# Expert numbers of a routing unit: compare, multiply and sum, against difference and least absolute value

## The reference

```python
q = (xt @ w_query).reshape(t, PEER_HEADS, 2, PEER_HALF)          # 8 heads, two halves of 128
s = jnp.einsum('thpd,hpnd->thpn', q, sub_keys)                   # 128 scores for each half
s_top, i_top = lax.top_k(s, PEER_TOPK)                           # 16 best keys of each half
cand = (s_top[:, :, 0, :, None] + s_top[:, :, 1, None, :]).reshape(t, PEER_HEADS, 256)
c_top, c_idx = lax.top_k(cand, PEER_TOPK)                        # 16 best sums
idx1 = jnp.take_along_axis(i_top[:, :, 0], c_idx // PEER_TOPK, axis=-1)
idx2 = jnp.take_along_axis(i_top[:, :, 1], c_idx % PEER_TOPK, axis=-1)
expert = idx1 * PEER_KEYS + idx2                                 # number of the expert
gate = jax.nn.softmax(c_top, axis=-1)
```

## Time and profile before

| | |
|---|---|
| median of 3 runs | 3614.72 us (3612.92 to 3615.78) |
| span of the profiled execution | 3610.9 us |
| time of the profiled execution | not listed apart from its span; the runs shown lie 2.0 to 4.9 us above that span |
| PE busy | 3447.2 us (95%) |
| DVE busy | 2815.0 us (78%) |
| ACT busy | 1079.8 us (30%) |
| POOL busy | 1422.8 us (39%) |

### The profile page before, as it was taken

One profiled execution on the slowest core, in us unless ns is written; L12 is line 12 of the kernel. 1 busy time (PEld: TensorE's weight loads), 2 busy tenths in 40 slices (PEclk: granted clock), 3 DMA queues, 4 the chain that ended last, 5 costly groups with the idle time before them and its releaser, 6 DMA issues.

```text
span 3610.9 us, 39997 instructions
## 1 busy us (share of the span) xinstructions
PE 3447.2 (95%) x11593; PEld 1976.1 (55%) x11593; DVE 2815.0 (78%) x6484; ACT 1079.8 (30%) x2721; POOL 1422.8 (39%) x1233
## 2 busy tenths in 40 slices
PE   7999999999997999768799999999999999999998
PEld 4666666777774566556344444444444444444443
DVE  2466686776774389899788888987898889888898
ACT  3233344544442222268221112111211121121212
POOL 1000000000001277500566565655666566655665
PEclk9999999999997999989899999999999999999999
DMA  3111013000002234247999999999999999999998
GB/s 112 30 36 35 0 32 109 23 23 29 29 35 114 50 60 91 34 139 203 394 393 377 393 380 392 379 380 356 394 372 387 386 397 377 375 394 377 390 376 340
DMA packets 313936, 829.65 MB, mean 230 GB/s; under 512 B 41504, under 2 KB 145056, under 8 KB 305056
## 3 DMA queue, kind: packets, MB, share of 16 engines
q0 software_dynamic: 165888, 537.01, 39.9%
q1 hardware_dynamic: 125104, 227.45, 17.4%
q10 hardware_dynamic: 22768, 63.18, 4.5%
HBM read 789.73 MB, written 37.81 MB: 229 GB/s over the span
## 4 chain that ended last, share of the span: by engine, by line
PE 46%; issue 5%; DVE 3%; DMA 2%; POOL 1%; ACT 0%; ACTq 0%; DVEq 0%; POOLq 0%
PE peer_ps_o L1971 23%; PE peer_ps_d L1958 20%; PE peer_ps_q L1888 2%; DMA peer_vr<-in_v_rows,peer_index 2%; DVE Y L2196 1%; POOL peer_vr L1863 0%; DVE peer_mt L2156 0%; DVE peer_mt L2160 0%; POOL peer_ur L1856 0%; DVE peer_ur L2185 0%; PE peer_ps_s L1903 0%; DMA peer_ur<-in_u_rows,peer_index 0%; DVE route_hit L1221 0%; DVE peer_chosen L1223 0%; DVE Y L2213 0%
## 5 line engine op out<-in xcount | busy, mean ns | idle before, releaser
L1856 POOL DMA_INDIRECT peer_ur<-in_u_rows,peer_index x512 | 566.1, 1106 | 600.1 <-DVE peer_ur L2185 418.7
L2196 DVE SCALAR_TENSOR_TENSOR Y<-peer_vr,osq,Y 128x1024 f32<-128x1024 f32 x512 | 656.7, 1283 | 100.2 <-DMA peer_vr<-in_v_rows,peer_index 99.8
L1863 POOL DMA_INDIRECT peer_vr<-in_v_rows,peer_index x512 | 588.3, 1149 | 324.9 <-issue 148.2
L2185 DVE SCALAR_TENSOR_TENSOR peer_ur<-peer_ur,Y 128x1024 f32<-128x1024 f32 x512 | 627.6, 1226 | 8.0 <-DMA peer_ur<-in_u_rows,peer_index 8.0
L1958 PE MATMUL peer_ps_d<-hnT,route_ut 128*128 128x512 f32 x1376 | 598.6, 592 | 0.7 <-ACT peer_vr L2031 0.7
L1971 PE MATMUL peer_ps_o<-hw,Y 128*128 128x512 f32 x1024 | 446.2, 595 | 14.8 <-DVE Y L2172 14.7
L1971 PE MATMUL peer_ps_o<-hnT,Y 128*128 128x512 f32 x1024 | 442.6, 592 | 0.0
L1958 PEld LDWEIGHTS peer_ps_d<-hnT,route_ut 128*128 128x128 f32 x1376 | 261.2, 190 | 328.6 <-issue 327.7
L1971 PEld LDWEIGHTS peer_ps_o<-hw,Y 128*128 128x128 f32 x1024 | 194.9, 191 | 257.5 <-issue 235.9
L1971 PEld LDWEIGHTS peer_ps_o<-hnT,Y 128*128 128x128 f32 x1024 | 193.5, 190 | 238.2 <-issue 238.0
L1958 PE MATMUL peer_ps_d<-hnT,peer_ut 128*128 128x512 f32 x672 | 297.3, 595 | 6.7 <-ACT Y L2039 6.7
(11 more groups left out here) (331 smaller groups left out, 5018.8 us busy)
## 6 DMA issues: line engine op xcount, KB each, us to landing
route_ut<-in_u_cols SPq DMA_DIRECT2D x86, 512.0 KB, 7.4
hw<-in_v_cols SPq DMA_DIRECT2D x16, 2048.0 KB, 11.0
peer_mt<-sel ACTq DMA_DIRECT2D x64, 512.0 KB, 9.2
hnT<-in_v_cols SPq DMA_DIRECT2D x16, 2048.0 KB, 13.6
peer_ut<-in_u_cols SPq DMA_DIRECT2D x42, 512.0 KB, 7.3
route_wk<-in_w_route ACTq DMA_DIRECT2D x14, 1024.0 KB, 7.8
hnT<-in_w_route SPq DMA_DIRECT2D x9, 1024.0 KB, 4.8
route_wk<-in_w_route SPq DMA_DIRECT2D x9, 1024.0 KB, 6.9
```

What stands on the lines that cost most here:

```text
L1856: pool.indirect_dma_start(ur[:, r % RING, :], None, u_rows, bass.IndirectOffsetOnAxis(ap=index[:, r // TOPK % 4, r % TOPK:r % TOPK + 1], a ...
L1863: pool.indirect_dma_start(vr[:, r % RING, :], None, v_rows, bass.IndirectOffsetOnAxis(ap=index[:, r // TOPK % 4, r % TOPK:r % TOPK + 1], a ...
L2185: nc.vector.scalar_tensor_tensor(out=ur[:, s, :], in0=ur[:, s, :], scalar=1.0, in1=Y[:, b, D:MIX], op0=ALU.mult, op1=ALU.mult, accum_out=d ...
L2196: nc.vector.scalar_tensor_tensor(out=hb, in0=vr[:, s, :], scalar=hid[:, c:c + 1], in1=hb, op0=ALU.mult, op1=ALU.add).then_inc(comb_done, 1)
```

## The change

The place of a candidate is now written into its number. `APART` is 2 x 128 x 128 = 32768, more than any expert number. Each key number gets a share added: for the first half 32768 times the place at which the key's row of candidates begins (`ROW_START`), for the second half 32768 times its rank. The sum of both is 32768 x place + expert number. `route_experts` then takes 32768 x chosen place less this number. Where the places agree, the absolute value is the expert number; everywhere else it is larger. A reduce by minimum with absolute value picks it out.

Per unit this has one operation over 16 x 54 elements and one reduce, where there were two and one. In `route_keys` two scalar_tensor_tensor over 16 elements stand for one multiply over 32. The buffers `count_u` (54 words) and `wide` go, `shift` (32 words) comes, `hit` is called `apart`. At the start of `mix_out`, 32 memsets of one element fill `shift` in place of two for `wide`, and one iota goes from POOL.

```diff
+ROW_START = [sum((v - u) * w for u, v, w in GRID if v <= i) + r * m for i, j, m in GRID for r in range(j - i)]
+APART = 2 * KEYS * KEYS
...
-        self.count_u = sb("count_u", [P, NCAND], U32)
-        self.wide = hw[:, FIRST_K * D + 4:FIRST_K * D + 6].unsqueeze(2)
-        self.hit = sb("hit", [P, TOPK, NCAND])
+        self.shift = sb("shift", [P, 2, TOPK])
+        self.apart = sb("apart", [P, TOPK, NCAND])
...
-    own.now(nc.vector.tensor_tensor(R.ti[:, 1], R.ix[:], R.wide.to_broadcast([P, 2, TOPK]), ALU.mult))
+    for p in range(2):
+        own.step(nc.vector.scalar_tensor_tensor(out=R.ti[:, 1, p, :], in0=R.ix[:, p, :], scalar=(float(KEYS), 1.0)[p],
+                                                in1=R.shift[:, p, :], op0=ALU.mult, op1=ALU.add))
+    own.hold()
...
 def route_experts(nc, dve, own, R, n, chosen):
-    own.now(nc.vector.tensor_tensor(R.hit[:], R.count_u[:].unsqueeze(1).to_broadcast([P, TOPK, NCAND]),
-                                    R.place[:].unsqueeze(2).to_broadcast([P, TOPK, NCAND]), ALU.is_equal))
-    own.now(nc.vector.tensor_tensor(R.hit[:], R.hit[:], R.ce[:, 1, :].unsqueeze(1).to_broadcast([P, TOPK, NCAND]),
-                                    ALU.mult))
-    return nc.vector.tensor_reduce(chosen, R.hit[:], AX.X, ALU.add)
+    own.now(nc.vector.scalar_tensor_tensor(out=R.apart[:], in0=R.place[:].unsqueeze(2).to_broadcast([P, TOPK, NCAND]),
+                                           scalar=float(APART),
+                                           in1=R.ce[:, 1, :].unsqueeze(1).to_broadcast([P, TOPK, NCAND]),
+                                           op0=ALU.mult, op1=ALU.subtract))
+    return nc.vector.tensor_reduce(chosen, R.apart[:], AX.X, ALU.min, apply_absolute_value=True)
...
-            nc.gpsimd.iota(R.count_u[:], pattern=[[1, NCAND]], base=0, channel_multiplier=0)
...
-            nc.vector.memset(R.wide[:, 0, :], float(KEYS))
-            own.now(nc.vector.memset(R.wide[:, 1, :], 1.0))
+            for a in range(TOPK):
+                nc.vector.memset(R.shift[:, 0, a:a + 1], float(APART * ROW_START[a]))
+                own.step(nc.vector.memset(R.shift[:, 1, a:a + 1], float(APART * a)))
```

## The result

Before: 3613.82 us (median of 4 runs). After: 3594.52 us (median of 4, 3591.34 to 3597.35). The ratio is 0.9945, 95% interval 0.9934 to 0.9957: 19.3 us less, where 3593 was forecast. After measured once more, beside other kernels, gave 3592.03 us and 0.9942 (0.9929 to 0.9956). The profiled execution of after has a span of 3590.6 us against 3610.9.

A forecast was written before the change was run, and what follows sets the result against it. DVE's late routing of the first blocks was taken to cause PE's 14.75 us wait. Savings of 20.0 + 1.8 = 21.8 us took the 3610.9 span to 3589.1; adding 3.8 around it gave 3592.9, forecast 3593, range 3589 to 3597 (chance 0.66).

The forecast's parts named there:

- The lookup: Each routing unit on DVE: one wide pass fewer, 1.09 us, less 0.09 for key numbers, net 1.00 us saved.
- Blocks 4 to 6: First routing stage: DVE's additions come earlier, 13.4 us at block 6, with PE setting the time from block 5.
- The gates of unit 27: On ACT, freed by DVE three units after block 6's addition: 16.4 us earlier, 1481.4 instead of 1497.75.
- PE's wait: At the x transpositions in the first routing stage: about 1.2 us stays of 14.75.
- The clock: PE's clock stays 1.00 behind the wait: 1.4 us back in projection 15, 0.6 in transpositions; may be nothing.
- The stage: First routing stage: block 7 taken up 18.0 us earlier, plus 2.0 in units 30 and 31, sum 20.0 us.
- Selection and expert stage: Selection gains zero, as DVE waits for ACT; in the expert stage PE's two waits for L2172 lose 0.9 each, 1.8.
- the forms (1): Rival in the lookup: the new reduce eats the saved pass, 3607 us (0.07) or no change (0.05); chance 0.12.
- the gathers: Rival in the expert stage: gather buffers move in memory and gathers lose speed, 3648 us at 10%; chance 0.04.
- rival 3: Expert stage: gather buffers free sooner, both waits for L2172 vanish, 10 us instead of 1.8: 3585 us; chance 0.05.
- Rival 2: PE's gap partly stays through ACT's order or a slow clock: 14 to 17 us instead of 21.8, 3599; chance 0.13.
- the signs named beforehand: Passes 1.06 and 1.05 us, additions within 0.5, PE's wait under 3, clock 1.00, stage 20 us shorter, L1246 waiting 2 longer.

The follow-up runs named there:

- Experiment 4: After with both wide passes of the lookup left out in the 32 units of the mixing stage (after, no lookup): 3588.80 us.
- Experiment 5: After with each block's first score ahead of the y transpositions, its copy ahead of square and y copies (after, score first): 3589.61 us.
- experiments 2, 6 and 8: Kernels of after with the x transpositions of blocks 4 and 5, or all but the first, behind score 15: 3584.99, 3584.86 and 3584.21 us.
- experiment 3: After with ACT's four x copies moved ahead of the gates of unit 27 (after, x copies first): 3591.36 us.
- experiment 1: Before with the new lookup in the mixing stage alone: 3597.63 us; in the expert stage alone: 3611.45 us.
- experiment 6: All moves: x transpositions behind score 15, first score early, gates of unit 31 before the copy of projection 16. On after 3584.86 us, on before 3597.11.
- after, one turn early: After with all moves of experiment 6, but the first of four x transpositions back in front of projection 15: 3584.21 us.
- after, x turned last: After with the x transpositions of blocks 4 and 5 and their copies moved behind score 15, query copy behind the root: 3584.99 us.
- after, expert load: After with the 864-wide pass done four times instead of once in the 32 units of the expert stage: 3631.13 us.
- before, x turned last: Before with the x transpositions of blocks 4 and 5 and their copies moved behind score 15, query copy behind the root: 3604.57 us.

## Why the prediction was right, and where its sizes were off

Times here are offsets, so that the 1.4 us of head start is in none of them.

*The lookup.* Predicted 1.00 us per unit. Where units follow each other directly, the distance from one to the next fell by 1.02 (8.36 to 7.34 us); over block 4 it is 0.96 a unit. The pass took 1054 ns where 1058 was put in, the reduce 1053 as put in, and the second key operation cost 0.07 us instead of 0.09. The Trainium skill's advice (VectorE: DVE Perf Modes, Rules for kernel authors) to minimize the number of operations would have given nothing here: the lookup and its key numbers are four operations still. By the trace the elements decide, 62.4 us of DVE's busy time in 64 units.

*Blocks 4 to 6.* Predicted: 6.0, 11.3 and 13.4 us earlier, with PE the limit from block 5 on. Measured: 5.8, 11.2 and 13.35. Experiment 4 shows the limit: at block 6 another 2.1 us per unit gives nothing at all.

*The gates of unit 27.* Predicted 16.4 us earlier; they came 14.6. The step that was mis-sized is "DVE gives them free three units later": in the trace of before DVE had waited 1.70 us for ACT's copy of the score behind the addition, and I carried that over. With PE early, ACT's y copies and the gates of unit 23 stand in front of it, and the wait is 3.39. Experiment 5 takes them away and the wait with them.

*PE's wait.* Predicted about 1.2 us left; 2.79 stayed, for the same reason.

*The clock.* Predicted: 1.00 stays, 2.0 us returned, "it may be nothing". The four transpositions did return 0.9 us, but projection 15 took 9.55 us, 1.1 more than before and not 1.4 less. This is the largest miss, 2.5 us in one term. The waits caused it: with no wait in front of it the same projection takes 7.07 (experiments 2, 6 and 8), and in experiment 3's one profiled execution also with 0.74 in place of 2.79.

*The stage.* 14.6 + 0.9 - 1.1 = 14.4 at block 7 (predicted 18.0), and 2.1 in units 30 and 31 (predicted 2.0): 16.5 against 20.0.

*Selection and expert stage.* Predicted 0 and 1.8; the profile has 2.3 from END on. The first PE wait lost 1.07 us (predicted 0.9), which experiment 1 confirms in both directions. The one near the end lost 1.6 in after, but it is 3.5 us with the new form in the expert stage alone, so its size is not the change's alone.

The rivals: neither the forms (1) nor the gathers (4; 388 GB/s in 1772 to 2132 us) lost anything. Of rival 3 nothing came: both waits for L2172 are still there, 5.89 and 1.44 us. Rival 2, a rest of the gap, was half right: ACT's order and a lower clock kept 3.5 us of it. Of the signs named beforehand, those of the passes, of the additions of blocks 5 and 6, of PE's longest wait (2.79) and of L1246 (1.8 us more) came true; the clock at 1.00 and a stage 20 us shorter did not.

The forecast of 3593 lay 1.5 under one median and 1.0 over the other. Part of that closeness is luck: the gain forecast was 21.8 us and 19.3 and 20.8 were measured, and the forecast started from a median of before of 3614.72, 0.9 and 1.9 us above those that after was then measured beside.

## What to carry to other kernels

When a faster engine hands the lead to another, read each small wait in the new order of events and not at its old length: here ScalarE's queue order made a wait of 1.70 us one of 3.39 as soon as TensorE led, and waits in front of a projection cost up to 2.5 us more through the clock. The order was not free before either: with it mended, before's waits for scores fell away too (experiment 6). The floor of the other engine can be read beforehand as the additions' distance when it runs full (52 to 53 us a block here), and it says how much the next saving is worth here: 19 us for the first microsecond per unit, 3 to 6 for the next two. A busy share of 0.86 is no slack of 14%: here the operation that TensorE waits for stands right behind the lookup, and 3.3 us more per unit cost 39 of 105 us.

## What was not expected of the hardware

Short waits in a row brought the clock down. These are the waits of PE between the x transpositions and the projection behind them, in every trace that has them in this place or, marked, in front of projection 16:

| kernel | waits, us | projection, us |
|---|---|---|
| after, x copies first | 0.74, 0.78, 0.69 | 7.07 |
| after, no lookup | 1.26, 0.78, 0.69 | 8.55 |
| after, score first | 1.26, 0.78, 0.69 | 8.68 |
| after, all moves (projection 16) | 1.77, 0.78, 0.69, 0.78 | 8.94 |
| after, one turn early (projection 16) | 1.86, 0.69, 0.78 | 9.44 |
| after, x turned last (projection 16) | 2.22, 0.78, 0.69, 0.78 | 8.53 |
| after, expert load | 2.75, 0.78, 0.69 | 9.26 |
| after | 2.79, 0.78, 0.69 | 9.55 |
| new form in the mixing stage alone | 2.81, 0.78, 0.69 | 9.25 |
| after, second time | 2.83, 0.78, 0.69 | 9.30 |
| before, all moves (projection 16) | 10.95, 0.78, 0.69, 0.78 | 9.21 |
| before | 14.75, 0.78, 0.69 | 8.46 |
| new form in the expert stage alone | 14.76, 0.78, 0.69 | 8.05 |
| before, x turned last (projection 16) | 15.83, 0.78, 0.69, 0.78 | 8.72 |

With a first wait of 0.74 us the projection kept its 7.07 us, and with 1.26 it took 1.5 us more. The first of these is one execution and the second two, so no limit between them is shown. Beyond that a longer wait does not mean a longer projection. The busy time by stretch says why, for after, for the kernel without the lookup, and for before:

```profile
1485.00:1491.50 6.50, 5.82 (x16) 4.79 (x17) 5.93 (x31) 1.19 (x2) 5.58 (x4) 0.50 0.23 4
```

```profile
1483.50:1486.50 3.00, 3.00 (x11) 2.43 (x10) 2.70 (x19) 0.60 (x1) 2.39 (x2) 0.50 0.19 8
```

```profile
1489.50:1506.00 16.50, 5.61 (x18) 4.34 (x19) 15.38 (x66) 3.97 (x11) 12.44 (x9) 0.50 0.19 2
```

Read in steps of half a microsecond, the clock is 1.00 on both sides of each stretch, with one mixed step at each edge. What counts is how much of the projection lies in such a stretch. In before the clock had fallen during the long wait and came back at about 1506.3, 2.8 us into the projection that began at 1503.50. In after it fell only at about 1484.8, among the transpositions, and came back at 1491.6, 5.0 us into the projection. As an estimate, a stretch at 0.50 costs half its length: 7.07 + 2.5 = 9.6 us for after, 7.07 + 1.4 = 8.5 for before, and 7.07 + 1.5 = 8.6 without the lookup (3.0 us), against 9.55, 8.46 and 8.55 measured. The Trainium skill (TensorE: Matmul & The Clock Gate, A second HAM failure mode: psum-queue depth-cycling) describes another kernel in which small idle times between groups of matmuls let the clock fall again and again. This stretch, four groups with a copy between each, resembles it; here the clock fell once, and with the first wait at 0.74 us it did not fall.
